# Final sum, norm and output of all tokens made during the last expert, its 160 rows merged and scattered on top

## The reference

```python
h = h + hybrid_mixer(rms_norm(h, norm_mix_w[l]), ...)
h = h + moe_ffn(rms_norm(h, norm_ffn_w[l]), router_w[l], router_b[l],
                gu_w[l], gu_b[l], dn_w[l], dn_b[l])
return rms_norm(h, norm_final_w)
# inside moe_ffn: 32 experts, each token goes to its top 4, softmax gates
x_glu = jnp.minimum(h[:, 0::2], SWIGLU_LIMIT)
x_lin = jnp.clip(h[:, 1::2], -SWIGLU_LIMIT, SWIGLU_LIMIT)
act = x_glu * jax.nn.sigmoid(SWIGLU_ALPHA * x_glu) * (x_lin + 1.0)
return act @ dn_w[e] + dn_b[e]
```

## Time and profile before

| | us |
|---|---|
| median of 3 runs | 2409.34 (2407.56 to 2410.25) |
| the profiled execution | 2407.89 |
| its span, first to last instruction | 2406.3 |
| PE busy | 2311.1 (96% of the span) |
| DVE busy | 815.0 (34%) |
| ACT busy | 451.9 (19%) |
| POOL busy | 326.4 (14%) |
| HBM traffic, mean over the span | 218 GB/s |

### The profile page before, as it was taken

One profiled execution on the slowest core, in us unless ns is written; L12 is line 12 of the kernel. 1 busy time (PEld: TensorE's weight loads), 2 busy tenths in 40 slices (PEclk: granted clock), 3 DMA queues, 4 the chain that ended last, 5 costly groups with the idle time before them and its releaser, 6 DMA issues.

```text
span 2406.3 us, 47150 instructions
## 1 busy us (share of the span) xinstructions
PE 2311.1 (96%) x18684; PEld 1713.2 (71%) x18685; DVE 815.0 (34%) x1936; ACT 451.9 (19%) x916; POOL 326.4 (14%) x340
## 2 busy tenths in 40 slices
PE   7999999799989999999999999999999999999994
PEld 4443444688844577887788778878887887788782
DVE  2466511466643432222222222222222222223222
ACT  3322100222233301111111111111111111111112
POOL 0000000111101221211111111112111211111121
PEclk9999999899999999999999999999999999999997
DMA  3011111411153276898698769777896898679784
GB/s 124 31 67 35 53 53 35 136 48 44 31 222 106 90 291 240 300 341 309 258 338 311 302 260 340 288 307 297 298 351 257 304 342 313 256 301 343 302 326 151
DMA packets 101072, 529.44 MB, mean 220 GB/s; under 512 B 25800, under 2 KB 50524, under 8 KB 76417
## 3 DMA queue, kind: packets, MB, share of 16 engines
q1 hardware_dynamic: 78960, 484.27, 51.6%
q0 software_dynamic: 22064, 44.50, 7.5%
HBM read 484.40 MB, written 40.05 MB: 218 GB/s over the span
## 4 chain that ended last, share of the span: by engine, by line
PE 91%; DVE 4%; DMA 2%; issue 1%; ACT 1%; SPq 0%; DVEq 0%; POOLq 0%; POOL 0%; ACTq 0%
PE ps L1533 38%; PE ps L1553 19%; PE ps L1182 13%; PE ps L1445 5%; PE ps L1563 2%; PE ps L1542 2%; PE ps L1355 2%; PE ps L1329 1%; PE ps L1351 1%; PE ps L1572 1%; DMA arena<-arena 1%; DVE arena L919 1%; PE ps L1213 1%; PE ps L1294 1%; PE ps L1518 0%
## 5 line engine op out<-in xcount | busy, mean ns | idle before, releaser
L1533 PEld LDWEIGHTS ps<-arena 128*128 128x128 f32 x7808 | 925.9, 191 | 16.4 <-issue 15.0
L1533 PE MATMUL ps<-arena 128*128 128x128 f32 (+2 forms) x7808 | 926.9, 281 | 1.1 <-ACT arena L802 1.1
L1553 PE MATMUL ps<-arena 128*128 128x512 f32 x1024 | 453.2, 595 | 0.0
L1182 PE MATMUL ps<-arena 128*128 128x512 f32 x832 | 361.8, 594 | 0.8 <-ACT arena L644 0.8
L1553 PEld LDWEIGHTS ps<-arena 128*128 128x128 f32 x1024 | 190.2, 190 | 221.2 <-issue 220.5
L1143 DVE TENSOR_SCALAR arena<-ps,arena 128x160 f32<-128x160 f32 x256 | 98.3, 384 | 619.9 <-PE ps L1533 536.5
L1182 PEld LDWEIGHTS ps<-arena 128*128 128x128 f32 x832 | 157.6, 190 | 202.4 <-issue 202.4
L811 ACT ACTIVATE arena<-arena 128x160 f32<-128x160 f32 x256 | 86.1, 336 | 832.1 <-DVE arena L1143 828.9
L582 POOL DMA_INDIRECT sum_s<-arena,idx_s x32 | 53.2, 1662 | 844.4 <-ACT arena L819 820.3
L1445 PE MATMUL ps<-arena 128*128 128x512 f32 x256 | 112.8, 594 | 2.1 <-DVE arena L1046 2.1
L1149 DVE SCALAR_TENSOR_TENSOR arena<-arena 128x160 f32<-128x160 f32 x256 | 83.2, 325 | 46.2 <-ACT arena L811 45.8
(11 more groups left out here) (231 smaller groups left out, 1883.4 us busy)
## 6 DMA issues: line engine op xcount, KB each, us to landing
arena<-gu_w SPq DMA_DIRECT2D x128, 2048.0 KB, 13.4
arena<-dn_w SPq DMA_DIRECT2D x64, 2048.0 KB, 14.0
arena<-dn_b SPq DMA_DIRECT2D x32, 512.0 KB, 16.1
arena<-w_in_t SPq DMA_DIRECT2D x26, 512.0 KB, 3.2
arena<-arena SPq DMA_DIRECT2D x32, 256.0 KB, 2.7
arena<-x SPq DMA_DIRECT2D x4, 1024.0 KB, 8.2
arena<-w_out SPq DMA_DIRECT2D x2, 2048.0 KB, 12.8
arena<-x SPq DMA_DIRECT2D x8, 512.0 KB, 6.3
```

The costliest lines, as they stand in the source:

```text
L1182: last = nc.tensor.matmul(ps[:, bank + h, :], win[:, slot, kt * P:(kt + 1) * P], xnT[:, kt, h * HALF:(h + 1) * HALF], start=kt == 0, stop= ...
L1533: last = nc.tensor.matmul(ps[:, f % 2, k * C:k * C + size], wslot[u][:, kt, o:o + P], xT[:, kt, 0:size], start=kt == 0, stop=kt == KT - 1, ...
L1553: last = nc.tensor.matmul(ps[:, 2 + h, :], actT[:, ft, 0:P], wslot[4 + h][:, ft, :], start=ft == 0, stop=ft == KT - 1)
```

## The change

Experts 0 to 30 run as before, the loops of DVE, ACT and POOL are one turn shorter, and expert 31 is written out behind them. SP, once the scatters of experts 0 to 30 have landed, loads the sums of all tokens (4 times 1 MB) into space that is free beside the weights. During the last four gate-up steps of expert 31 ACT squares these eight tiles; DVE multiplies tiles 0 to 2 by the norm weight and later scales tiles 3 to 7 (weight and factor in one), ACT scales tiles 0 to 2; SP writes all eight to the output. For the tokens of expert 31 these output rows lack its part. So POOL also gathers the sums of just these rows (`rows`, `rows2`) by the expert's own list, DVE adds gate times bias, then gate times each half of the down matmul straight from PSUM, ACT squares the result, the factor is made (for the 32 tokens in pieces by a small matmul with a constant, `stack_all`, that adds the four pieces' sums), DVE and ACT scale the rows, and POOL scatters them onto the output with two plain scatters, after all eight tiles have been written. The old tail stays only for the case of further rounds, where it is run in the flag's branch. Four small loads of 32 KB (the norm weight in pieces) are added on SP ahead of the experts, and the constant table grows from 593 to 689 columns.

The core of the diff (new branches for further rounds, renamed semaphores and DVE's SwiGLU step, only moved into a function, left out):

```diff
+        sums = [at(112 + 8 * g, GROUP, D) if g < 3 else at(56, GROUP, D) for g in range(GROUPS)]
+        rows, rows2 = at(178, D), at(182, PW)
+        nw3 = at(186, D)
+        nw3p = at(183, PW)
+        sqj3 = at(190, D)
+        ACT_TILES = 3
...
+            for g in range(PIECES):
+                sp.dma_start(nw3p[g * REST:(g + 1) * REST, :], normw_d[1][0:REST, g * PW:(g + 1) * PW]).then_inc(s_par, 16)
...
+            def sums_in():
+                for g in range(GROUPS):
+                    lo, hi = g * GROUP, (g + 1) * GROUP
+                    sp.dma_start(sums[g], acc_d[lo * P:hi * P, :].rearrange("(t p) n -> p t n", p=P)).then_inc(s_x[g], 16)
+
+            def tile_out(t):
+                sp.dma_start(out[t * P:(t + 1) * P, :], sum_of(t)).then_inc(s_out[t % 2], 16)
+
+            def experts_sp(r):
+                if not isinstance(r, int):
+                    expert_weights(0, r)
+                    return
+                expert_weights(1, r)
+                sp.wait_ge(s_sc, 32 * (E - 1))
+                sums_in()
+                for k in range(TT - ACT_TILES):
+                    if k < ACT_TILES:
+                        sp.wait_ge(s_sd, RT + k + 1)
+                        tile_out(k)
+                    sp.wait_ge(s_o, k + 1)
+                    tile_out(ACT_TILES + k)
+                for k in range(2):
+                    sp.wait_ge(s_out[k], 16 * TT // 2)
...
+                gather(E, 0, E)
+                pool.wait_ge(s_sc, 32 * n)
+                pool.sem_inc(s_scr, 1)
+                list_in(n, 0, idx_s, idx_s2, s_is)
+                pool.wait_ge(s_is, 32 * n + 32)
+                pool.indirect_dma_start(rows, None, acc_d, bass.IndirectOffsetOnAxis(ap=idx_s[:, 0:1], axis=0),
+                                        bounds_check=T + TRASH - 1, oob_is_err=False).then_inc(s_ls, 16)
+                pool.indirect_dma_start(rows2, None, acc_pieces, bass.IndirectOffsetOnAxis(ap=idx_s2[:, 0:1], axis=0),
+                                        bounds_check=PIECES * (T + TRASH) - 1, oob_is_err=False).then_inc(s_ls, 16)
+                for k in range(2):
+                    pool.wait_ge(s_out[k], 16 * TT // 2)
+                pool.wait_ge(s_sd, RT + ACT_TILES + 1)
+                pool.wait_ge(s_o, TT - ACT_TILES + 1)
+                pool.indirect_dma_start(out, bass.IndirectOffsetOnAxis(ap=idx_s[:, 0:1], axis=0), Yt, None,
+                                        bounds_check=T - 1, oob_is_err=False).then_inc(s_sc, 16)
+                pool.wait_ge(s_o, TT - ACT_TILES + 2)
+                pool.indirect_dma_start(out_pieces, bass.IndirectOffsetOnAxis(ap=idx_s2[:, 0:1], axis=0), Y2, None,
+                                        bounds_check=PIECES * T - 1, oob_is_err=False).then_inc(s_sc, 16)
...
+            def square_sum(t, loads, before):
+                act.wait_ge(s_x[t // GROUP], 16 * loads)
+                act.wait_ge(s_sq2, before)
+                nc.scalar.activation(sqj3, sum_of(t), ACT.Square, accum_out=stat3[:, 0, t:t + 1]).then_inc(s_sq2, 1)
+
+            def last_expert_act():
+                n = E - 1
+                for f in range(KT):
+                    glu_sigmoid(n, f)
+                    if f >= KT - GROUPS:
+                        for t in range(GROUP * (f - KT + GROUPS), GROUP * (f - KT + GROUPS + 1)):
+                            square_sum(t, 2, TT + t)
+                act.wait_ge(s_ms2, TT + 1)
+                nc.scalar.activation(stat3[:, 1, :], stat3[:, 1, :], ACT.Sqrt).then_inc(s_rt2, 1)
+                act.wait_ge(s_nm, RT + 1)
+                for t in range(ACT_TILES):
+                    act.wait_ge(s_h, TT + t + 1)
+                    nc.scalar.activation(sum_of(t), sum_of(t), ACT.Copy, scale=stat3[:, 2, t:t + 1]).then_inc(s_sd, 1)
+                copy_xT(E)
+                act.wait_ge(s_sq2, 2 * TT)
+                act.wait_ge(s_ye, 3 * n + 7)
+                nc.scalar.activation(sqj3[:, 0:HALF], rows[:, 0:HALF], ACT.Square, accum_out=rows_sq[:, 0:1]).then_inc(s_sq2, 1)
+                act.wait_ge(s_ye, 3 * n + 8)
+                act.wait_ge(s_sq2, 2 * TT + 1)
+                nc.scalar.activation(sqj3[:, 0:PW], rows2, ACT.Square, accum_out=rows_sq[:, 2:3]).then_inc(s_sq2, 1)
+                act.wait_ge(s_ye, 3 * n + 9)
+                act.wait_ge(s_sq2, 2 * TT + 2)
+                nc.scalar.activation(sqj3[:, 0:HALF], rows[:, HALF:D], ACT.Square, accum_out=rows_sq[:, 1:2]).then_inc(s_sq2, 1)
+                act.wait_ge(s_ms2, TT + 2)
+                nc.scalar.activation(rows_rt[:, :], rows_rt[:, :], ACT.Sqrt).then_inc(s_rt2, 1)
+                act.wait_ge(s_nm, RT + 2)
+                act.wait_ge(s_h, TT + ACT_TILES + 1)
+                nc.scalar.activation(Yt[:, HALF:D], Yt[:, HALF:D], ACT.Copy, scale=rows_rs[:, 0:1]).then_inc(s_sd, 1)
+                act.sem_inc(s_yr, 3)
...
+                def weighted_tile(t):
+                    dve.wait_ge(s_sq2, TT + t + 1)
+                    nc.vector.tensor_tensor(sum_of(t), sum_of(t), nw3, ALU.mult).then_inc(s_h, 1)
+
+                for f in range(KT):
+                    glu(n, n, f)
+                    if f >= KT - ACT_TILES:
+                        weighted_tile(f - KT + ACT_TILES)
+                dve.wait_ge(s_ls, 16 * TT * TOPK + 32)
+                dve.wait_ge(s_db, 16 * (PIECES + 1) * (n + 1))
+                dve.wait_ge(s_is, 32 * n + 32)
+                nc.vector.scalar_tensor_tensor(out=rows, in0=dnb, scalar=gate, in1=rows, op0=ALU.mult, op1=ALU.add)
+                nc.vector.scalar_tensor_tensor(out=rows2, in0=dnb2, scalar=gate2, in1=rows2, op0=ALU.mult, op1=ALU.add)
+                dve.wait_ge(s_sq2, 2 * TT)
+                nc.vector.tensor_scalar(stat3[:, 1, :], stat3[:, 0, :], 1.0 / D, RMS_EPS, ALU.mult, ALU.add
                                         ).then_inc(s_ms2, 1)
-                dve.wait_ge(s_rt2, TT + g + 1)
-                ch.link(nc.vector.reciprocal(stat3[:, 2, w], stat3[:, 1, w]))
-                for t in range(g * GROUP, (g + 1) * GROUP):
-                    nc.vector.scalar_tensor_tensor(out=fin[:, t, :], in0=hf[:, t, :], scalar=stat3[:, 2, t:t + 1],
-                                                   in1=nw3, op0=ALU.mult, op1=ALU.mult).then_inc(s_o, 1)
+                dve.wait_ge(s_rt2, TT + 1)
+                nc.vector.reciprocal(stat3[:, 2, :], stat3[:, 1, :]).then_inc(s_nm, 1)
+                dve.wait_ge(s_nm, RT + 1)
+                for t in range(ACT_TILES, TT):
+                    scaled_tile(t)
+
+                dve.wait_ge(s_par, (2 + PIECES) * 16)
+                dve.wait_ge(s_scr, n + 1)
+                dve.wait_ge(s_dn, 3 * n + 1)
+                nc.vector.scalar_tensor_tensor(out=rows[:, 0:HALF], in0=ps[:, 2, :], scalar=gate, in1=rows[:, 0:HALF],
+                                               op0=ALU.mult, op1=ALU.add).then_inc(s_ye, 1)
+                dve.wait_ge(s_ye, 3 * n + 7)
+                nc.vector.tensor_tensor(Yt[:, 0:HALF], rows[:, 0:HALF], nw3[:, 0:HALF], ALU.mult)
+                dve.wait_ge(s_dn, 3 * n + 2)
+                nc.vector.scalar_tensor_tensor(out=rows2, in0=ps[:, 6, 0:PW], scalar=gate2, in1=rows2,
+                                               op0=ALU.mult, op1=ALU.add).then_inc(s_ye, 1)
+                dve.wait_ge(s_ye, 3 * n + 8)
+                nc.vector.tensor_tensor(Y2, rows2, nw3p, ALU.mult)
+                dve.wait_ge(s_dn, 3 * n + 3)
+                nc.vector.scalar_tensor_tensor(out=rows[:, HALF:D], in0=ps[:, 3, :], scalar=gate, in1=rows[:, HALF:D],
+                                               op0=ALU.mult, op1=ALU.add).then_inc(s_ye, 1)
+                dve.wait_ge(s_ye, 3 * n + 9)
+                nc.vector.tensor_tensor(Yt[:, HALF:D], rows[:, HALF:D], nw3[:, HALF:D], ALU.mult).then_inc(s_h, 1)
+                dve.wait_ge(s_rank, TT + 2)
+                nc.vector.tensor_scalar(rows_rt[:, 1:2], ps[:, 0, 0:1], 1.0 / D, RMS_EPS, ALU.mult, ALU.add)
+                dve.wait_ge(s_sq2, 2 * TT + 3)
+                ch.link(nc.vector.tensor_tensor(rows_sq[:, 0:1], rows_sq[:, 0:1], rows_sq[:, 1:2], ALU.add))
+                nc.vector.tensor_scalar(rows_rt[:, 0:1], rows_sq[:, 0:1], 1.0 / D, RMS_EPS, ALU.mult, ALU.add
+                                        ).then_inc(s_ms2, 1)
+                dve.wait_ge(s_rt2, TT + 2)
+                nc.vector.reciprocal(rows_rs[:, :], rows_rt[:, :]).then_inc(s_nm, 1)
+                dve.wait_ge(s_nm, RT + 2)
+                nc.vector.tensor_scalar(Yt[:, 0:HALF], Yt[:, 0:HALF], rows_rs[:, 0:1], None, ALU.mult).then_inc(s_o, 1)
+                nc.vector.tensor_scalar(Y2, Y2, rows_rs[:, 1:2], None, ALU.mult).then_inc(s_o, 1)
...
+                    pe.wait_ge(s_sq2, 2 * TT + 2)
+                    nc.tensor.matmul(ps[:, 0, 0:1], stack_all, rows_sq[:, 2:3], start=True, stop=True).then_inc(s_rank, 1)
```

154 lines of the change are left out of this document (95 added, 59 removed).

## The result

The kernel with the change takes 2392.92 us (median of 4 runs, 2389.15 to 2393.26); the kernel before, run beside it, 2408.7 (2407.56 to 2410.25). The ratio is 0.9929, 95% interval 0.9917 to 0.9942. Two later sets of runs of the same code gave 2391.75 and 2390.31, with the kernel before beside them at 2410.08 and 2409.35. So it is faster by 15.8 us in the first set and by 18.3 and 19.0 in the later ones, where the forecast was 2387.5 and a span 21.0 us shorter. The profiled execution is one of 2392.92 us, with a span of 2391.4.

The account below looks back on a forecast made before the run. PE bounds the experts; the change targets the 34.3 us after its last matmul. Steps through the final scatter end the span at 2385.3, 21.0 less: 2386.9, or 2388.3 on the median's scale; middle named 2387.5, range 2383.3 to 2393.

Parts of the forecast that it names:

- rival A: Expert 31's list takes 12.0 us to load, rows come at 2368.1, DVE's queue moves by 5.1: time 2392.4, chance 0.15.
- S: Mark in expert 31: start of its twelve gate-up matmuls of 160 columns; 2354.93 in the profile before, 2358.25 after.
- Squares against PE: Expert 31's last gate-up steps: ACT's squares delay the sigmoids and stall PE 0.6 to 1.7 us, taken as 1.1.
- List and rows: Expert 31's list, loaded beside the sums, lands at 2357; POOL issues the gather 1.0 later; rows in at 2363.0.
- DVE's queue: DVE waits for gathered rows until 2363.0, then bias, factor, five tiles and both row halves; merged rows ready at 2376.7.
- Last tile: Output writes from 2366.5: 10.4 us at bandwidth plus 1.5 to land, last at 2378.4; the final scatter waits 1.7.
- POOL's issue: Before the final scatter: 1.58 us after the last tile lands until POOL issues, giving 2380.0.
- The scatter's landing: Final scatter: 1.4 us to the second issue and 3.6 to landing, as the gather, so 2385.0; upper bound 1.96 and 5.08.
- The end: After the final scatter lands: 0.3 us to the end of the span, as before, so 2385.3.
- B: Sums' loads spread by further traffic make ACT hold PE longer in expert 31: bound 4 us, 2391, chance 0.07.
- D: Better tail: list in 2.1 us, PE stall at most 0.6, POOL's issue 0.9; time 2384.8, chance 0.06.
- C: New straight code fetched late, 2.7 us per gap: one gives 2389.6; one or two 0.10, enough to cancel or reverse 0.02.

Follow-up runs that it names:

- list_first: The changed kernel, but POOL loads expert 31's list before it issues the last gather of tokens: median 2387.24 us, ratio 0.9910.
- sp_waits: The changed kernel, but SP instead of POOL waits for the last scatter to land: median 2388.54 us, ratio 0.9913.

## Why the prediction was right, and what it missed

Faster was right, and the range held the time, but with luck: the first median lies 0.1 us inside its upper bound of 2393, and the range was drawn up to there for rival A, a late list, which did not come. 2387.5 was 5.4 us below the first median and 2.8 below the lowest of the later ones. Each step, set against S (forecast with S 2354.93, measured with 2358.25):

- **Order and releasers, right.** L501 follows the landed scatter at once (2348.94, S − 9.3; forecast 2345.6, S − 9.3). DVE idles at L1296 for the rows, L641 waits for the written tiles, the DMA share is near 1 while they are written, PE's loop keeps its pace.
- **Squares against PE.** Forecast 1.1 us, between 0.6 and 1.7; measured 0.1, and 0.1 to 0.6 over the kernel's four profiles. The landings were as in the earlier trace rows (4.8, 8.3 and 11.6), but the sixth sigmoid ran 0.4 us sooner (S − 2.1, forecast S − 1.7) and the seventh step was ready at S + 1.6, just when PE wanted it, not at S + 2.2. The error had no weight, since the end hung on DVE.
- **List and rows, right by two errors.** The list took 5.61 us, not 6.9, and the token gather ahead of it didn't lengthen it (list_first). That speaks against the reading by which it would land when nearly all sums had passed: it landed at 2359.1, and the last sums, issued at 2350.4, took 11.6 us, to 2362.0. POOL needed 1.58 us to issue instead of 1.0, and the gather 4.15 instead of 3.6. Rows in at S + 8.1 by both, which is luck. But the forecast took this wait as given; 2.8 us of the end could be had for the order of two loads.
- **DVE's queue, right to 0.1 us.** L1310 at S + 16.4, the merged rows ready at S + 21.7 (2379.99), forecast S + 21.8.
- **Last tile.** Forecast S + 23.5, measured S + 24.0 (2382.3): 0.6 too early. The 1.5 us of the forecast behind the transfer came from tiles written one by one, at 2.6 to 3.5 us each; here they took 2.7 to 5.7.
- **POOL's issue.** 0.9 behind the tiles' landing, not 1.58: 0.7 too long. Bounds for it were in the rows only one-sided.
- **The scatter's landing.** Forecast 3.6 from the gather; measured 4.6, and 3.0 to 4.6 over all profiles. Against the upper bound's 5.08 the choice of the lower was right, its size some 0.5 us short on the mean of the kernel's four.
- **The end.** The step that failed: "0.3 us to the end as now". In before the last thing to end was a tile write that SP waited for, while POOL had drained from 2382.2 on, 1.70 us, out of sight. The change makes POOL the last to wait, and its drain of 1.87 us comes behind the landing. 2.3 us instead of 0.3; sp_waits shows it. The drain and SP's last branch in before:

```profile
L119 POOLq DRAIN  x1: 1702/1702/1702, 2382.2 to 2382.2; - x1
L119 SPq COMPARE_BRANCH  x1: 41/41/41, 2405.9 to 2405.9; - x1
```

- **Ahead of S.** The forecast carried before's single profile to the new program unchanged, and that one was 0.5 to 0.9 us quicker up to S than the two other profiles with the old tail: 3.3 us in this profile, 1.8 between the means of all profiles with the old tail and with the new.

In sum 0.6 − 0.7 + 1.0 + 2.0 − 0.1 behind S and 3.3 ahead of it are the 6.1 us between 2385.3 and 2391.4. Rival A (a late list) did not come; its price was also mis-added, 5.1 us on 2386.9 are 2392.0 and not 2392.4. B came as far as 0.1 to 0.6 us, and of D only POOL's 0.9 us. C did not come: neither DVE nor ACT waited on "issue" for as much as 1 us in expert 31. That agrees with the rule that fetching ahead is sequential (the Trainium skill, Runtime: NRT & Kernel Launch, section Instruction fetch mechanics).
